# Eleven low parts of weight pieces moved from VectorE to GpSimd, with a wait of TensorE for each piece, in a two-block transformer kernel

## The chip, the cores and the metric

The kernel runs on one core of one Trainium2 chip, as one launch. The metric is the device time of the launch in microseconds. The kernel before took 1385.69 us (median of three runs, 1382.89 to 1385.78).

## What is computed

256 tokens of width 1024 go through two blocks. The first has four SwiGLU feed-forward layers (each added with factor 0.5), an mLSTM mixer after the first and an NSA attention mixer (compressed, selected and window branches over a shared K/V) after the third. The second has a forgetting-attention mixer (FOX) and a sparse attention mixer with an indexer (DSA), each followed by a layer norm. All is float32. Cut to the order of the work:

```python
x = x + 0.5 * swiglu(rmsnorm(x))              # ffn0
x = x + mlstm(rmsnorm(x) @ w_in) @ w_out      # mlstm, mlstm_out
x = x + 0.5 * swiglu(rmsnorm(x))              # ffn1
kv = rmsnorm(x) @ kv_w                        # kv, compressed during ffn2
x = x + 0.5 * swiglu(rmsnorm(x))              # ffn2
x = x + nsa(rmsnorm(x) @ w_in, kv) @ w_out    # nsa, nsa_out
x = x + 0.5 * swiglu(rmsnorm(x))              # ffn3
x = layer_norm(alpha * x + fox(x))            # fox, fox_out
x = layer_norm(alpha * x + dsa(x))            # dsa, dsa_out
```

## The kernel before

Every product with a weight is done in three products of a rounded type: a value v is split into a high part (v rounded) and a low part (v minus the high part), and x w is taken as x_lo w_hi + x_hi w_lo + x_hi w_hi (lines 658, 659, 661 in `product`, 689, 690 and 696 where the first products go ahead of the low part of x). The weights, 207 pieces of up to 128 x 2048, come through one ring of 7 slots. For each piece SyncE loads `raw` (waiting until TensorE has used the piece 7 before it), ScalarE writes the high part `whi` (`hi`, line 1472, semaphore `hi_done`), and VectorE subtracts it, `wlo = raw - whi` (`lo`, line 1987, semaphore `lo_done`). TensorE waits for `lo_done` and, after its last product with a piece, raises `used`.

The order on each engine is written out by hand. On ScalarE and on VectorE `split_to(p)` stands between the other steps and makes the high or low parts of all pieces below p that are still to be made, in order, so a low part delays what comes after it on VectorE, and a later step delays the low parts behind it. GpSimd has little to do: it issues the parameter loads at the start, masks the mLSTM decay (AFFINE_SELECT, line 623), clears pads (MEMSET, lines 627 to 640), and issues the loads of the layer-norm parameters (lines 636, 637) and of `wuk` and `wuv` (lines 641, 642).

Pieces are counted within their stage from 0. The places that the change touches:

- mlstm_out, 4 pieces. VectorE makes their low parts between the steps of the end of the mLSTM mixer: `m_weights` (lines 2291, 2293, one input in PSUM), `numerators_in` (2306 to 2309), `og_gain` (2322), `heads` (2330, eight small products per token tile), after which TensorE transposes the heads (line 705) and multiplies them with the four pieces.
- nsa_out, 4 pieces. Pieces 0 and 1 are split between the two token tiles of q: VectorE takes the root (lines 1999 to 2008) and norms q (`q_normed`, line 2505), then TensorE transposes q (line 1198). Pieces 2 and 3 are split at the end of the NSA attention.
- dsa, 12 pieces (chunks 0 to 5 of two pieces each), then dsa_out, 4 pieces (so 13 is the second piece of dsa_out). Chunks 0 to 2 are multiplied for token tile 0 while the layer norm of tile 1 (lines 2169 to 2186) still runs; in the middle of chunk 2 TensorE transposes tile 1 of h (line 678). Then come chunks 0 to 2 for tile 1, the transposes of `wuk` (1381) and of qi (1389), chunk 3, the transposes of ki and ckv (1395, 1396) and kr (1400), the index products (1411) and chunk 4. On VectorE, beside these: the rope of qi (lines 2690 to 2695), the root of ckv and the ropes of kr and ki up to the copy in line 2719, the copy of kr in line 2725, then index scores and `choose` (2750 to 2755, a top-k by repeated maxima). Chunk 5 fills TensorE while VectorE masks and scales the scores; its result goes through `silu_gate` (line 2602).

TensorE waited for a whole chunk at once (`pe.wait_ge(lo_done, end)` ahead of both its pieces) in `chunk`, `n_chunk` and the first three chunks of dsa, and for each piece by itself in the feed-forward layers and the output products.

Of the kernel before, what the change touches and what calls it, by code (L numbers as in the profile page):

```python
# [15 lines left out]
F32 = mybir.dt.float32  # L16
# [86 lines left out]
def program(nc, a, out):  # L103
# [34 lines left out]
    with ExitStack() as ctx:  # L138
# [185 lines left out]
        head_sq = sem("head_sq")  # L324
        og_ps = sem("og_ps")
        m_decay = sem("m_decay")
        og_act = sem("og_act")
# [272 lines left out]
        def _(pool):  # L600
            def load_rows(r, n, src):
                pool.dma_start(rowsb[r:r + n, :], src).then_inc(params_in, 16)

            load_rows(R_MIX, 16, a["mix_norm"].rearrange("l (k p) -> (l k) p", p=P))
            load_rows(R_KV, 8, a["kv_norm"].rearrange("(k p) -> k p", p=P))
# [13 lines left out]
            for j in range(HEADS // 2):  # L619
                pool.wait_ge(m_decay, j + 1)  # L620
                for blk in (slice(0, P), slice(256, 384)):
                    two_heads = m_E[:, 2 * j:2 * j + 2, blk]
                    pool.affine_select(out=two_heads, in_=two_heads, compare_op=ALU.is_ge, fill=0.0, base=0,
                                       pattern=[[0, 2], [1, P]], channel_multiplier=-1).then_inc(m_diag, 1)

            pool.wait_ge(h_part, h_at("mlstm_out", 1, 1))
            pool.memset(KB[:, :, :], 0.0).then_inc(pads_ready, 1)
# [4 lines left out]
            pool.memset(FL[:, :, :, :].bitcast(F32), 0.0).then_inc(pads_ready, 1)  # L632

            for i, name in enumerate(["fox_out", "dsa_out"]):
                pool.wait_ge(z_ready, 2 * (i + 2))
                pool.dma_start(LNB[:, 0, :], a["ln_g_2"][i:i + 1, :].to_broadcast([P, D])).then_inc(ln_in, 16)
                pool.dma_start(LNB[:, 1, :], a["ln_b_2"][i:i + 1, :].to_broadcast([P, D])).then_inc(ln_in, 16)
                if i == 0:
                    pool.wait_ge(h_part, h_at("ln0", 1, 1))
                    pool.memset(d_wukr[:, :, 0:32], 0.0).then_inc(pads_ready, 1)  # L640
                    pool.dma_start(d_wukr[:, :, 32:128], a["dsa_w_uk_2"].rearrange("h c n -> c h n")).then_inc(wuk_in, 16)
                    pool.dma_start(d_wuv[:, :, :], a["dsa_w_uv_2"].rearrange("h c d -> c h d")).then_inc(wuk_in, 16)


        @block.tensor
        def _(pe):
# [34 lines left out]
            def first_products(o, name, t, banks, los=(0, 0)):  # L681

                for i, (w, ks) in enumerate(banks):
                    if los[i]:
                        pe.wait_ge(lo_done, los[i])
                    pe.wait_ge(turned_hi, 4 * turns.index(name) + 2 * t + w + 1)
                    for j, (k, wh, wl) in enumerate(ks):
                        xh = XH[:, k, t * P:t * P + P]
                        mm(o, xh, wl, start=i == 0 and j == 0, stop=False, skip_group_check=True)  # L689
                        mm(o, xh, wh, start=False, stop=False, skip_group_check=True)  # L690
# [36 lines left out]
            def ffn(f, during=None):  # L727
# [25 lines left out]
                def in_products(i, t):  # L753
                    if i == 0:
                        first_half(t)
                        return
                    p = p0 + in_piece(f, i)
                    pe.wait_ge(gated, 2 * (n0 + i - 1) + t + 1)
                    for half in range(2):
                        if t == 0:  # L760
                            pe.wait_ge(lo_done, p + half + 1)
                        wh, wl = parts(p + half, 4)
                        last = product(PS[:, 4 + t, :],
                                       [(XH[:, 4 * half + k, t * P:t * P + P], XL[:, 4 * half + k, t * P:t * P + P],
                                         wh[:, k, :], wl[:, k, :]) for k in range(4)], start=half == 0, stop=half == 1)
                        if t == 1:
                            last.then_inc(used, 1)
                        elif half == 1:
                            last.then_inc(a_ready, 1)
# [8 lines left out]
                def out_step(i, between=None):  # L778
                    p = p0 + out_of(f, i)
                    pe.wait_ge(gl_done, n0 + i + 1)  # L780
                    pe.wait_ge(lo_done, p + 1)
                    last = i == NI - 1
                    out_piece(p, 0, GHz if last else GH, GLz if last else GL, i == 0, last, then_turns[name], between)
# [21 lines left out]
            def chunk(stage, c, then=None):  # L805
# [13 lines left out]
                ps = [(end - 1, 8)] if whole else [(end - 2, 4), (end - 1, 4)]  # L819
                pe.wait_ge(lo_done, end)  # L820
                if c == 0:
# [5 lines left out]
                    for t in range(NT):  # L827
                        o = PS[:, b0 + t, 0:n]
                        first_products(o, stage, t, banks)
                        if t == 0:  # L830
# [10 lines left out]
                for m in tiles:  # L841
                    for i, (p, kn) in enumerate(ps):
                        wh, wl = parts_n(p, kn, n)
                        if kind == A_CHUNK:
# [21 lines left out]
            def out_part(name, t, i):  # L866

                p = first_piece[name] + i
                if t == 0:
                    pe.wait_ge(lo_done, p + 1)  # L870
                if name == "mlstm_out":
# [177 lines left out]
            def og_products(c, t, bank):  # L1049

                n, end = stages["mlstm"][1][c][2], chunk_end("mlstm", c)
                for i, p in enumerate((end - 2, end - 1)):
                    if t == 0:
                        pe.wait_ge(lo_done, p + 1)
                    wh, wl = parts_n(p, 4, n)
# [53 lines left out]
            def blocks(kv):  # L1109
# [3 lines left out]
                for i in range(2):  # L1113
                    p = cmp_piece(kv) + i
                    pe.wait_ge(lo_done, p + 1)
                    wh, wl = parts(p, 8)
# [49 lines left out]
            def n_chunk(t, c):  # L1166

                n, end = stages["nsa"][1][c][2], chunk_end("nsa", c)
                o = PS[:, n_bank(t, c), 0:n]
                if t == 0:  # L1170
                    pe.wait_ge(lo_done, end)
                if c == 0:
                    banks = []
                    for w in range(2):
                        wh, wl = parts_n(end - 2 + w, 4, n)
                        banks.append((w, [(4 * w + k, wh[:, k, :], wl[:, k, :]) for k in range(4)]))
                    first_products(o, "nsa", t, banks)
                    for w, ks in banks:
# [3 lines left out]
                else:  # L1182
                    ps = [(end - 2, 4), (end - 1, 4)] if c == 1 else [(end - 1, 8)]
                    for i, (p, kn) in enumerate(ps):
                        wh, wl = parts_n(p, kn, n)
                        last = product(o, [(XH[:, kn * i + k, t * P:t * P + P], XL[:, kn * i + k, t * P:t * P + P],
# [170 lines left out]
            for t in range(NT):  # L1357
                for c in range(3):
                    n, end = stages["dsa"][1][c][2], chunk_end("dsa", c)
                    if t == 0:  # L1360
                        pe.wait_ge(lo_done, end)
                    for i in range(2):
                        if t == 0 and c == 2 and i == 1:
                            for w in range(2):
                                turn_h("dsa", 1, w)
                        wh, wl = parts_n(end - 2 + i, 4, n)
                        pe.wait_ge(x_ready, x_at("dsa", t, 4 * i + 3))
# [90 lines left out]
        def _(act):  # L1458
# [445 lines left out]
            x_hi("dsa", 0)  # L1904
            split_to(first + 5)
            deviation("ln0", 1)
# [66 lines left out]
        def _(dve):  # L1973
# [16 lines left out]
            def split_to(p_end):  # L1990
                for p in range(split[0], min(p_end, NP)):
                    lo(p, pieces[p][1] if pieces[p] else PIECE)
                split[0] = max(split[0], min(p_end, NP))
# [840 lines left out]
```

## Time and profile before

| | |
|---|---|
| median of three runs | 1385.69 us |
| lowest, highest | 1382.89, 1385.78 us |
| profiled execution, its own time | 1382.88 us |
| its span | 1381.2 us |
| mean granted TensorE clock | 0.979 of full speed |
| busy: TensorE, VectorE, ScalarE, GpSimd | 1302.3, 877.3, 616.9, 21.7 us |
| low parts on VectorE (line 1987) | 207, 459.4 us in all |

The profile is one execution, recorded by the hardware. Busy time is the time in which an engine works on an instruction; waiting for a semaphore is not busy. Times on the timeline count from the start of the span. In a timeline row stand the start in us, the length in us, engine, line, operation, the tile written and the tiles read, the shape, and how many equal instructions the row merges; then, in brackets, how long the engine was idle before it and who released it. The tile name `arena` covers most of the mixers' tiles.

### The profile page before, as it was taken

The numbers are of one execution on the slowest core, as the hardware profiler recorded it, in microseconds if no ns is written. First come the engines' busy times: TensorE is split into PE (matmuls) and PEld (weight loads), VectorE is DVE, ScalarE is ACT, GpSimd is POOL, SyncE is SP. The second block draws the span as 40 slices with busy tenths as digits, with TensorE's granted clock in tenths as the row PEclk, the third lists the DMA queues.
The fourth block names the chain that finished last, engine by engine and source line by source line (L and its number), as shares of the span: only waits on it lengthen the run. The fifth ranks groups of instructions, "written<-read, shape, count | busy, mean of one in ns | idle before, by whom it ended". The sixth has DMA issues, their size and how long they took to land.

```text
span 1381.2 us, 16655 instructions
## 1 busy us (share of the span) xinstructions
PE 1302.3 (94%) x6797; PEld 1099.3 (80%) x6797; DVE 877.3 (64%) x1329; ACT 616.9 (45%) x836; POOL 21.7 (2%) x36
## 2 busy tenths in 40 slices
PE   5999999879999999999999988989999999989887
PEld 4888888778788888878888865878888999868765
DVE  5555557595655557685866587665555675577664
ACT  5444446434344445534444465534443354434531
POOL 1000000100000000000000000000000000000000
PEclk9999999999999999999999999999999999999899
DMA  8665545333555555547564230355556765246001
GB/s 277 222 193 190 184 155 191 112 126 124 178 193 190 193 190 170 173 155 235 183 213 159 104 110 1 122 166 194 191 192 131 184 193 175 63 152 244 32 0 61
DMA packets 158780, 218.18 MB, mean 158 GB/s; under 512 B 8224, under 2 KB 110960, under 8 KB 158704
## 3 DMA queue, kind: packets, MB, share of 16 engines
q1 hardware_dynamic: 156848, 212.56, 47.8%
q0 software_dynamic: 1376, 3.71, 0.9%
q8 instruction: 54, 0.88, 0.3%
q10 hardware_dynamic: 480, 0.85, 0.2%
q14 instruction: 22, 0.18, 0.0%
HBM read 216.04 MB, written 1.05 MB: 157 GB/s over the span
## 4 chain that ended last, share of the span: by engine, by line
PE 82%; DVE 12%; ACT 3%; issue 2%; DMA 1%; ACTq 0%; POOL 0%; DVEq 0%
PE PS L658 23%; PE PS L659 22%; PE PS L661 22%; DVE wlo L1987 3%; PE PS L775 1%; PE PS L689 1%; PE PS L690 1%; ACT whi L1472 1%; PE PS L678 1%; PE PS L974 1%; DVE XL L2026 1%; ACT XH L1494 1%; PE PS L696 1%; PE PS L1258 1%; PE PS L1244 1%
## 5 line engine op out<-in xcount | busy, mean ns | idle before, releaser
L1987 DVE TENSOR_TENSOR wlo<-raw,whi 128x2048 fp32r<-128x2048 f32 (+3 forms) x207 | 459.4, 2230 | 125.1 <-ACT whi L1472 124.4
L1472 ACT ACTIVATE whi<-raw 128x2048 fp32r<-128x2048 f32 (+3 forms) x207 | 383.0, 1865 | 60.9 <-DMA raw<-in_fox_w_in_dram 33.5
L658 PE MATMUL PS<-whi,XL 128*128 128x512 f32 (+3 forms) x992 | 389.0, 393 | 21.6 <-DVE scr L2088 7.5
L659 PE MATMUL PS<-wlo,XH 128*128 128x512 f32 (+3 forms) x992 | 382.0, 386 | 0.0
L661 PE MATMUL PS<-whi,XH 128*128 128x512 f32 (+3 forms) x992 | 265.2, 384 | 0.0
L658 PEld LDWEIGHTS PS<-whi,XL 128*128 128x128 f32 x992 | 188.7, 190 | 58.6 <-DVE scr L2088 8.6
L659 PEld LDWEIGHTS PS<-wlo,XH 128*128 128x128 f32 x992 | 188.8, 190 | 33.2
L661 PEld LDWEIGHTS PS<-whi,XH 128*128 128x128 f32 x992 | 185.8, 190 | 35.8
L1526 ACT ACTIVATE scr<-PS,rn 128x256 f32<-128x256 f32 x88 | 41.7, 474 | 226.7 <-PE PS L661 224.0
L658 PE MATMUL PS<-whi,GL 128*128 128x512 f32 x320 | 125.4, 392 | 0.0
L659 PE MATMUL PS<-wlo,GH 128*128 128x512 f32 x320 | 124.6, 389 | 0.0
L1531 ACT ACTIVATE GH<-PS 128x512 fp32r<-128x512 f32 x40 | 23.9, 598 | 175.9 <-PE PS L775 175.9
L2085 DVE SCALAR_TENSOR_TENSOR scr<-PS,rn,scr 128x256 f32<-128x256 f32 x88 | 42.5, 482 | 91.4 <-ACT scr L1526 91.4
L661 PE MATMUL PS<-whi,GH 128*128 128x512 f32 x320 | 98.7, 390 | 0.0
L658 PE MATMUL PS<-XH,wlo 128*128 128x256 f32 x320 | 83.4, 291 | 3.3 <-DVE wlo L1987 3.3
L2094 DVE TENSOR_TENSOR GL<-PS,GH 128x512 fp32r<-128x512 f32 x40 | 27.7, 692 | 87.4 <-ACT GH L1531 87.4
L659 PE MATMUL PS<-XL,whi 128*128 128x256 f32 x320 | 82.5, 289 | 0.0
L661 PEld LDWEIGHTS PS<-whi,GH 128*128 128x128 f32 x320 | 60.1, 188 | 12.6
L659 PEld LDWEIGHTS PS<-wlo,GH 128*128 128x128 f32 x320 | 60.1, 188 | 12.1
L658 PEld LDWEIGHTS PS<-whi,GL 128*128 128x128 f32 x320 | 60.1, 188 | 12.2
L658 PEld LDWEIGHTS PS<-XH,wlo 128*128 128x128 f32 x320 | 63.5, 198 | 5.3 <-issue 5.2
L659 PEld LDWEIGHTS PS<-XL,whi 128*128 128x128 f32 x320 | 63.5, 198 | 0.0
(369 smaller groups left out, 1379.0 us busy)
## 6 DMA issues: line engine op xcount, KB each, us to landing
raw<-in_ffn_w_in_dram SPq DMA_DIRECT2D x176, 512.0 KB, 4.8
raw<-in_ffn_w_out_dram SPq DMA_DIRECT2D x88, 512.0 KB, 4.9
raw<-in_fox_w_in_dram SPq DMA_DIRECT2D x24, 512.0 KB, 7.8
raw<-in_a_w_in_dram SPq DMA_DIRECT2D x16, 512.0 KB, 4.4
raw<-in_dsa_w_in_dram SPq DMA_DIRECT2D x16, 512.0 KB, 5.6
raw<-in_kv_w_dram SPq DMA_DIRECT2D x12, 512.0 KB, 4.1
raw<-in_fox_w_in_dram SPq DMA_DIRECT2D x12, 344.0 KB, 5.2
raw<-in_a_w_out_dram SPq DMA_DIRECT2D x8, 512.0 KB, 4.8
```

The lines of the kernel that those rows point to most:

```text
L658: mm(o, xl, wh, start=start and i == 0, stop=False, skip_group_check=True)
L659: mm(o, xh, wl, start=False, stop=False, skip_group_check=True)
L661: last = mm(o, xh, wh, start=False, stop=stop and i == len(terms) - 1, skip_group_check=True)
L678: last = tr(PS[:, turn_bank(name, t, w), k * P:k * P + P], h[:, t, (4 * w + k) * P:(4 * w + k) * P + P], ident)
L689: mm(o, xh, wl, start=i == 0 and j == 0, stop=False, skip_group_check=True)
L690: mm(o, xh, wh, start=False, stop=False, skip_group_check=True)
L1472: A(whi[:, p % SLOTS, 0:n], raw[:, p % SLOTS, 0:n], ACT.Copy).then_inc(hi_done, 1)
L1526: A(ffe[:, t, :], PS[:, 4 + t, 0:FC], ACT.Sigmoid, scale=rn[:, t:t + 1]).then_inc(exp_done, 1)
L1531: A(to[:, :, :].rearrange("p k t -> p (k t)"), PS[:, 6, :], ACT.Copy).then_inc(gh_done, 1)
L1987: V.tensor_tensor(wlo[:, p % SLOTS, 0:n], raw[:, p % SLOTS, 0:n], whi[:, p % SLOTS, 0:n].bitcast(F32), ALU.subtract).then_inc(lo_done, 1)
L2085: V.scalar_tensor_tensor(out=g, in0=PS[:, 4 + t, 0:FC], scalar=rn[:, t:t + 1], in1=e, op0=ALU.mult, op1=ALU.mult).then_inc(silu_step, 1)
L2094: V.tensor_tensor(to[:, :, :], two(PS[:, 6, :]), hi_[:, :, :].bitcast(F32), ALU.subtract)\
```

## The change

GpSimd makes the low parts of eleven pieces: 1, 2 and 3 of mlstm_out, 0, 1 and 3 of nsa_out, and 5, 7, 9, 11 and 13 of dsa and dsa_out. It uses the same subtraction, from a helper `lo` of its own, and raises a semaphore of its own, `lo_pool`. VectorE's `split_to` skips these pieces. `lo_of(p)` gives, for a piece, which semaphore to wait for and its value. TensorE now waits for each piece by itself everywhere. ScalarE makes the high part of dsa piece 5 ahead of the squares of the layer norm's tile 1 instead of after them (`split_to(first + 6)`).

In GpSimd's order the mlstm_out pieces stand after the masks of the decay and ahead of the clearing of KB and VB, the nsa_out pieces ahead of the first layer-norm loads, dsa piece 5 between those loads and the wait for the first layer norm, and the last four after the loads of `wuk` and `wuv`.

```diff
+        lo_pool = sem("lo_pool")
+        pool_pieces = {"mlstm_out": (1, 2, 3), "nsa_out": (0, 1, 3), "dsa": (5, 7, 9, 11, 13)}
+        on_pool = sorted(first_piece[name] + i for name, part in pool_pieces.items() for i in part)
+
+        def lo_of(p):
+
+            if p in on_pool:
+                return lo_pool, on_pool.index(p) + 1
+            return lo_done, p + 1 - sum(1 for q in on_pool if q < p)
...
+            def lo(name, i):
+
+                p = first_piece[name] + i
+                n = pieces[p][1] if pieces[p] else PIECE
+                pool.wait_ge(hi_done, p + 1)
+                pool.tensor_tensor(wlo[:, p % SLOTS, 0:n], raw[:, p % SLOTS, 0:n], whi[:, p % SLOTS, 0:n].bitcast(F32),
+                                   ALU.subtract).then_inc(lo_pool, 1)
...
+            for i in pool_pieces["mlstm_out"]:
+                lo("mlstm_out", i)
             pool.wait_ge(h_part, h_at("mlstm_out", 1, 1))
...
+            for i in pool_pieces["nsa_out"]:
+                lo("nsa_out", i)
             for i, name in enumerate(["fox_out", "dsa_out"]):
                 pool.wait_ge(z_ready, 2 * (i + 2))
...
                 if i == 0:
+                    lo("dsa", pool_pieces["dsa"][0])
                     pool.wait_ge(h_part, h_at("ln0", 1, 1))
...
+                    for j in pool_pieces["dsa"][1:]:
+                        lo("dsa", j)
...
                 ps = [(end - 1, 8)] if whole else [(end - 2, 4), (end - 1, 4)]
-                pe.wait_ge(lo_done, end)
...
-                        first_products(o, stage, t, banks)
+                        first_products(o, stage, t, banks, (0, 0) if t else (end, 0) if whole else (end - 1, end))
...
                     for i, (p, kn) in enumerate(ps):
+                        if m == 0:
+                            pe.wait_ge(*lo_of(p))
...
             for t in range(NT):
                 for c in range(3):
                     n, end = stages["dsa"][1][c][2], chunk_end("dsa", c)
-                    if t == 0:
-                        pe.wait_ge(lo_done, end)
                     for i in range(2):
                         if t == 0 and c == 2 and i == 1:
                             for w in range(2):
                                 turn_h("dsa", 1, w)
+                        if t == 0:
+                            pe.wait_ge(*lo_of(end - 2 + i))
...
             x_hi("dsa", 0)
-            split_to(first + 5)
+            split_to(first + 6)
             deviation("ln0", 1)
...
             def split_to(p_end):
                 for p in range(split[0], min(p_end, NP)):
+                    if p in on_pool:
+                        continue
                     lo(p, pieces[p][1] if pieces[p] else PIECE)
```

`n_chunk` is changed as `chunk` is, and the other waits of TensorE for `lo_done` become waits for `lo_of` of the same piece.

## Rows read from the trace of the kernel before

**Rows 1.** The page: busy time, share of the span and instructions

```profile
PE 1302.3 (94%) x6797; PEld 1099.3 (80%) x6797; DVE 877.3 (64%) x1329; ACT 616.9 (45%) x836; POOL 21.7 (2%) x36
```

**Rows 2.** TensorE's waits: line, released by, us in total, times, longest

```profile
PE PS L658 <- DVE wlo L1987: 10.1, 3, 5.7
```

**Rows 3.** Timeline of GpSimd, mLSTM mixer, 258 to 263 us

```profile
258.32 0.76 POOL L623 TENSOR_SCALAR_AFFINE_SELECT arena<-arena 128x256 f32<-128x256 f32 x2 [221.63 <-DVE arena L2275]
...
260.38 2.01 POOL L623 TENSOR_SCALAR_AFFINE_SELECT arena<-arena 128x256 f32<-128x256 f32 x1
```

**Rows 4.** Timeline of VectorE, mLSTM mixer, 249 to 264 us

```profile
249.52 3.40 DVE L1987 TENSOR_TENSOR wlo<-raw,whi 128x1536 fp32r<-128x1536 f32 x2
...
260.37 1.76 DVE L1987 TENSOR_TENSOR wlo<-raw,whi 128x1536 fp32r<-128x1536 f32 x1 [0.42 <-ACT whi L1472]
262.05 1.96 DVE L1987 TENSOR_TENSOR wlo<-raw,whi 128x1536 fp32r<-128x1536 f32 x1
```

**Rows 5.** Timelines of ScalarE, VectorE and TensorE ahead of mlstm_out

```profile
301.15 1.90 ACT L1472 ACTIVATE whi<-raw 128x2048 fp32r<-128x2048 f32 x1
...
301.28 1.23 DVE L2322 TENSOR_TENSOR arena<-arena 128x1024 f32<-128x1024 f32 x1
...
304.77 2.18 DVE L2330 SCALAR_TENSOR_TENSOR xs<-xs,rr,arena 128x128 f32<-128x128 f32 x8
...
307.01 1.97 PE L705 MATMUL PS<-con,xs 128*128 128x128 f32 x8 [4.50 <-DVE xs L2330]
```

**Rows 6.** Timelines of ScalarE, VectorE and TensorE at the norm of q, NSA

```profile
782.62 1.90 ACT L1472 ACTIVATE whi<-raw 128x2048 fp32r<-128x2048 f32 x1
...
784.79 0.18 DVE L2008 SCALAR_TENSOR_TENSOR rr<-rt,ry 128x16 f32<-128x16 f32 x1
785.00 1.23 DVE L2505 TENSOR_TENSOR xs<-xs,rr 128x1024 f32<-128x1024 f32 x1
...
789.40 1.03 PE L1198 MATMUL PS<-con,xs 128*128 128x128 f32 x8
```

**Rows 7.** Timelines, DSA chunk 2; last a stretch's busy times, granted clock, DMA share, GB/s

```profile
1222.06 2.29 DVE L1987 TENSOR_TENSOR wlo<-raw,whi 128x2048 fp32r<-128x2048 f32 x1
...
1225.60 0.16 DVE L2174 TENSOR_TENSOR lns<-lns 128x1 f32<-128x1 f32 x1
...
1229.71 1.42 DVE L2186 SCALAR_TENSOR_TENSOR h<-xs,rr,arena 128x512 f32<-128x512 f32 x2
...
1233.50 0.80 PE L658 MATMUL PS<-whi,XL 128*128 128x512 f32 x1 [5.73 <-DVE wlo L1987]
...
1237.03 1.09 PE L661 MATMUL PS<-whi,XH 128*128 128x512 f32 x4
...
1240.68 1.08 PE L661 MATMUL PS<-whi,XH 128*128 128x512 f32 x4
...
1234.00:1238.00 4.00, 4.00 (x13) 3.09 (x13) 0.00 (x0) 0.00 (x0) 0.00 (x0) 0.63 0.70 191
```

**Rows 8.** Timelines of ScalarE, VectorE and TensorE, DSA from 1248 to 1271 us

```profile
1248.78 1.92 ACT L1472 ACTIVATE whi<-raw 128x2048 fp32r<-128x2048 f32 x1 [6.39 <-DMA raw<-in_dsa_w_in_dram]
...
1257.26 3.71 ACT L1472 ACTIVATE whi<-raw 128x2048 fp32r<-128x2048 f32 x2
...
1251.46 0.21 DVE L2690 TENSOR_TENSOR arena<-arena,con 128x64 f32<-128x64 f32 x1
...
1257.81 0.28 DVE L2708 CUSTOM_DVE_ANT_0 arena<-arena 128x128 f32<-128x128 f32 x1
...
1264.34 0.29 DVE L2719 COPY arena<-arena 128x256 f32<-128x256 f32 x1
...
1267.02 1.07 PE L661 MATMUL PS<-whi,XH 128*128 128x512 f32 x4
...
1270.17 3.80 PE L1411 MATMUL PS<-arena 64*128 64x128 f32 x24 [1.43 <-DVE arena L2725]
```

**Rows 9.** Timeline of TensorE at DSA chunk 5

```profile
1306.12 0.55 PE L658 MATMUL PS<-XH,wlo 128*128 128x256 f32 x1 [3.32 <-DVE wlo L1987]
```

More of the change, by code:

```diff
@@ L684, in first_products @@
                     if los[i]:
-                        pe.wait_ge(lo_done, los[i])
+                        pe.wait_ge(*lo_of(los[i] - 1))
                     pe.wait_ge(turned_hi, 4 * turns.index(name) + 2 * t + w + 1)
@@ L760, in in_products @@
                         if t == 0:
-                            pe.wait_ge(lo_done, p + half + 1)
+                            pe.wait_ge(*lo_of(p + half))
                         wh, wl = parts(p + half, 4)
@@ L780, in out_step @@
                     pe.wait_ge(gl_done, n0 + i + 1)
-                    pe.wait_ge(lo_done, p + 1)
+                    pe.wait_ge(*lo_of(p))
                     last = i == NI - 1
@@ L842, in chunk @@
                     for i, (p, kn) in enumerate(ps):
+                        if m == 0:
+                            pe.wait_ge(*lo_of(p))
                         wh, wl = parts_n(p, kn, n)
@@ L869, in out_part @@
                 if t == 0:
-                    pe.wait_ge(lo_done, p + 1)
+                    pe.wait_ge(*lo_of(p))
                 if name == "mlstm_out":
@@ L1053, in og_products @@
                     if t == 0:
-                        pe.wait_ge(lo_done, p + 1)
+                        pe.wait_ge(*lo_of(p))
                     wh, wl = parts_n(p, 4, n)
@@ L1114, in blocks @@
                     p = cmp_piece(kv) + i
-                    pe.wait_ge(lo_done, p + 1)
+                    pe.wait_ge(*lo_of(p))
                     wh, wl = parts(p, 8)
@@ L1176, in n_chunk @@
                         banks.append((w, [(4 * w + k, wh[:, k, :], wl[:, k, :]) for k in range(4)]))
-                    first_products(o, "nsa", t, banks)
+                    first_products(o, "nsa", t, banks, (0, 0) if t else (end - 1, end))
                     for w, ks in banks:
@@ L1184, in n_chunk @@
                     for i, (p, kn) in enumerate(ps):
+                        if t == 0:
+                            pe.wait_ge(*lo_of(p))
                         wh, wl = parts_n(p, kn, n)
@@ L1359, in _ @@
                     n, end = stages["dsa"][1][c][2], chunk_end("dsa", c)
-                    if t == 0:
-                        pe.wait_ge(lo_done, end)
                     for i in range(2):
@@ L1365, in _ @@
                                 turn_h("dsa", 1, w)
+                        if t == 0:
+                            pe.wait_ge(*lo_of(end - 2 + i))
                         wh, wl = parts_n(end - 2 + i, 4, n)
```

## The prediction

> **What bounds the kernel now.** I read the page first. TensorE is busy 94% of the span [rows 1], so only what makes TensorE wait, or lets it start earlier, can move the end. Next I read the table of waits for TensorE [rows 2]: it waits for `wlo`, the low part of a weight piece, three times in the whole kernel for 10.1 us at that line. Two of the three lie in the DSA stage, 5.73 us before the products at 1233.50 [rows 7] and 3.32 us before those at 1306.12 [rows 9]; the third is in ffn0, which the change leaves alone. VectorE makes the low part of every piece; the change takes eleven from it, and nine of these have no TensorE wait behind them. Then I read the timelines around each of the eleven, for what VectorE and TensorE do while GpSimd would be at work.
>
> **What GpSimd and VectorE do to each other.** The trace shows it once, clearly. Two AFFINE_SELECTs of 128x256 took 0.76 us together at 258.32, 0.40 each with a start every 0.36, but the one at 260.38 took 2.01 us [rows 3]. VectorE's subtraction of two SBUF tensors ran from 260.37 to 262.13. GpSimd ended at 262.39, 0.26 us later, and the next VectorE subtraction, recorded from 262.05, took 1.96 us where two of the same shape took 3.40 us together, 1.70 each [rows 4]. So the two engines excluded each other for whole instructions, and took turns: GpSimd got in between two VectorE instructions that stood back to back. Of the 0.40 us some 0.13 comes before the exclusion (0.40 less 0.26). The Trainium skill (SBUF — State Buffer, "Who interferes with whom") says the same: a VectorE instruction with two SBUF inputs and a GpSimd instruction that reads SBUF lock each other out, the later one for all of the earlier. By that rule, the trace agrees, a GpSimd subtraction stops every two-input VectorE instruction that comes up while it runs, and the change would lose time; without it, it would gain, as in rival (a).
>
> **Price of one GpSimd subtraction.** No row shows one. From below: VectorE's own, 2.29 us [rows 7]. From above: by the 0.36 us from start to start of the pair [rows 3], eight times (2048/256) and doubled for the second input, 5.8 us. I take 4.5: the 0.27 us of the 0.40 that follow the dispatch make 1.05 ns an element for one input, twice that for two, times 2048, is 4.3, plus 0.13. It is nearest to the rows of GpSimd itself. The Trainium skill (GPSIMD Engine Reference, "Elementwise — side-by-side cycle accounting") gives 4497 ns for a two-input add of this size; the sum would be the same.
>
> **Part 1, mlstm_out (pieces 1, 2, 3).** Removed: three subtractions of VectorE. The first brings the chain to the heads forward by about 1 us, after which it waits for TensorE; piece 2 runs beside `og_gain` of tile 0 (line 2322, two SBUF inputs) and takes most of that back. I set the two at nothing. Piece 3 becomes ready on ScalarE at 303.05; ScalarE waits there for TensorE, which is the microsecond ahead, so about 302.1; `og_gain` of tile 1 is then just running [rows 5], GpSimd follows it at about 303.1 and holds to 307.6. The eight head products of tile 1 (line 2330, two SBUF inputs, start 304.77) wait for that: they start 2.9 us late, and TensorE's transposes at 307.01, which already wait 4.50 us for them, come 2.9 us late. TensorE has nothing else queued there. Sum **+2.9**; between -1.0 (no exclusion) and +4.3 (GpSimd in ahead of `og_gain`).
>
> **Part 2, nsa_out (pieces 0, 1, 3).** ScalarE has piece 0 ready at 784.52 [rows 6]. GpSimd would be in at about 784.7, VectorE's last small step of the root (line 2008, two SBUF inputs) is due at 784.79 and the norm of q (line 2505) at 785.00. GpSimd holds to 789.2, VectorE does its 0.18 us step, GpSimd takes its turn with piece 1 to 793.9, and the norm ends at 795.1 instead of 786.2. TensorE asks for it at 789.40: **+5.7**. All hangs on 0.3 us: if GpSimd comes later than 785.00, the norm is ahead of it and the cost is nothing. Piece 3 hides behind TensorE's products of pieces 0 to 2. The two subtractions that VectorE loses here stood before a wait of it, so nothing is gained.
>
> **Part 3, dsa piece 5, with its own wait and the earlier high part.** Before, TensorE stood from 1227.77 to 1233.50, for both halves of chunk 2. Now it does the half that is ready (piece 4, from 1222.06 [rows 7], done at 1224.35) in 2.7 us of the gap, and then waits for the layer norm of tile 1 (line 2186, first half written at 1230.4). GpSimd starts piece 5 at 1224.35 and holds to 1228.85; the layer norm's line 2174 (two SBUF inputs, 1225.60) starts 3.25 us late and all behind it. TensorE resumes at 1233.7, turns h, and does the second half in 4.6 us at the lower clock, which is what the first half took after the old wait (1233.50 to 1238.12; the granted clock is 0.63 from 1234 to 1238, part at 1.2 and part at 2.4 GHz). Chunk 2 ends about 1239.6 (1233.7, a transpose of 0.9 and 4.6, with part of it overlapped) where it ended at 1241.76: **-2.2**. Without exclusion: -6.
>
> **Part 4, dsa pieces 7, 9, 11.** Piece 7 is ready on ScalarE at 1250.7 [rows 8], now 2.2 earlier, so GpSimd holds the port from 1248.7 to 1253.2, and the rope of qi (line 2690, now 1251.46, with part 3 at 1249.3) waits: 1.5 of the 2.2 us are lost, **+1.5**. Pieces 9 and 11: ScalarE makes high parts 9 to 11 back to back from 1257.26 [rows 8] (the row has the first two; 9 is the first, 11 the third), so GpSimd has two subtractions nearly end to end, 1258.6 to 1263.1 and, after one VectorE step, to 1267.8. From 1257.8 to 1264.3 [rows 8] VectorE runs the chain of small two-input instructions (root and ropes) that ends in line 2719 at 1264.34. 5.2 us of it are left at 1258.6, so it ends at 1273. TensorE finishes chunk 3 at 1267.4 and needs it: with the one subtraction left to VectorE there (2.3 us) and the copies up to line 2725 (1.1 us) its index products start at 1276.4, not 1270.17. This step alone costs **+6.9** (6.2 over the old time plus the 0.7 that parts 3 and 4 still had).
>
> **Part 5, the wait at chunk 5.** VectorE subtracted piece 11 just before, and TensorE waited 3.32 us [rows 9]. GpSimd has it ready long before. Piece 13 then holds the port during `choose(1)` and costs 0.5 at the gate that follows. **-2.8.**
>
> **Sum.** +2.9 +5.7 -2.2 +1.5 +6.9 -2.8 = +12.0 us. The profiled execution took 1382.9 us (span 1381.2 and 1.7 around it), so 1394.9; it is 2.8 below the median of the runs shown, 1385.69. As I don't know which of the two the next runs will be like, I forecast in the middle, 1384.3 + 12.0, rounded to **1396**. Its bounds: at 5.8 us a piece each of the seven blocks counted above is 1.3 us longer, +9; a lower clock of TensorE after the two new waits of over 5 us would add 1.8 each, the difference of the two halves in part 3 (4.6 and 2.8). At 2.3 us a piece the blocks nearly close: +0.6 +1.2 -4.4 +2 -2.8 = -3.4, which is inside the range below. With 4 to 5 us a piece the case has 1390 to 1405.
>
> **Rivals.** (a) *No exclusion for long GpSimd instructions*: the port is shared in small portions, so the blocks vanish. Then -1.0, 0, -6, -1.0 (VectorE has one subtraction fewer before line 2725, where TensorE waited 1.43 us [rows 8]) and -3.3, sum -11.3: **1373**. For it: the exclusion of VectorE by GpSimd is only shown for 0.26 us. Against it: GpSimd was shut out for all 1.76 us of a VectorE instruction. It is the case on the faster side. (b) *The double blocks miss*: GpSimd enters 0.3 us later at 785 and the pair 9 and 11 does not get a second turn. Then +2.9, 0, -0.7, +2.3, -2.8: **1386**, no change. It decides at line 2505. (c) *One of the two double blocks happens*: +6 to +7, **1391**. (d) *GpSimd takes well over 5.8 us*: pieces come late for TensorE itself and it ends above 1405.
>
> **How the numbers follow.** The forecast's case 0.42, (c) 0.18, (d) 0.04, (b) 0.11, (a) 0.25. A measurement of this kernel tells some 0.2%, 2.8 us, from no change, so (b) is half "same", and of (c) nearly all is slower: slower 0.65, same 0.09, faster 0.26. The range has to leave out no more than 0.2; the upper cases from 1384 hold 0.72, so it reaches into (a) to its slower half: 1375 to 1405. The forecast's case alone has 1390 to 1405.
>
> **What would show it.** In the profile after: eleven GpSimd TENSOR_TENSOR of 4.3 to 4.7 us; records of lines 2505 (or 2008), 2174, 2330 and the small steps before 2719 that last 3 us and more where they took 0.2 to 1.2; TensorE waiting for line 2505 near 789, and for line 2719 near 1268; the waits for `wlo` gone from the DSA stage. If two-input VectorE instructions keep their times beside a running GpSimd subtraction, the forecast is wrong and (a) holds.

## Result, and the profile after

The changed kernel takes 1398.07 us (median of ten runs, 1391.16 to 1403.32) against 1388.28 (ten runs, 1382.89 to 1392.70): ratio **1.0075, interval 1.0049 to 1.0102**. It is slower, by 10 us. The profiled execution took 1394.36 us, its span is 1392.6, its mean granted clock 0.972. The prediction had 1396 (1375 to 1405).

The first row of the page of the kernel after answers to [rows 1], and the row of costs beside it is GpSimd's:

```profile
PE 1305.6 (94%) x6797; PEld 1102.0 (79%) x6797; DVE 884.0 (63%) x1318; ACT 617.4 (44%) x836; POOL 73.7 (5%) x47
...
L619 POOL TENSOR_TENSOR wlo<-raw,whi 128x2048 fp32r<-128x2048 f32 x11 | 51.8, 4721 | 334.8 <-ACT whi L1498 334.8
```

VectorE lost eleven subtractions (207 at 459.4 us before, 196 at 436.6 now, so 22.8 us of work) and is busy for 6.7 us *more*. So its other instructions take 29.5 us longer (6.7 + 22.8). The timelines show which. First GpSimd's eleven subtractions (seven rows; two of them hold a pair):

```profile
278.28 4.90 POOL L619 TENSOR_TENSOR wlo<-raw,whi 128x2048 fp32r<-128x2048 f32 x1 [1.65 <-ACT whi L1498]
287.32 4.55 POOL L619 TENSOR_TENSOR wlo<-raw,whi 128x2048 fp32r<-128x2048 f32 x1 [4.14 <-ACT whi L1498]
302.36 5.04 POOL L619 TENSOR_TENSOR wlo<-raw,whi 128x2048 fp32r<-128x2048 f32 x1 [10.48 <-ACT whi L1498]
...
786.14 9.06 POOL L619 TENSOR_TENSOR wlo<-raw,whi 128x2048 fp32r<-128x2048 f32 x2 [160.45 <-ACT whi L1498]
...
1232.85 4.90 POOL L619 TENSOR_TENSOR wlo<-raw,whi 128x2048 fp32r<-128x2048 f32 x1 [17.89 <-ACT whi L1498]
...
1265.47 9.18 POOL L619 TENSOR_TENSOR wlo<-raw,whi 128x2048 fp32r<-128x2048 f32 x2 [5.18 <-ACT whi L1498]
...
1322.59 4.65 POOL L619 TENSOR_TENSOR wlo<-raw,whi 128x2048 fp32r<-128x2048 f32 x1 [47.93 <-ACT whi L1498]
```

(Two more, of pieces nsa_out 3 and dsa 7, start at 871.84 and 1255.69.) Then VectorE's timeline in the same stretches. Each row answers to one of [rows 5 to 8], where the same instruction took 2.18, 0.18, 1.23, 0.16 and 0.21 us:

```profile
305.05 4.33 DVE L2358 SCALAR_TENSOR_TENSOR xs<-xs,rr,arena 128x128 f32<-128x128 f32 x8
...
786.15 4.63 DVE L2036 SCALAR_TENSOR_TENSOR rr<-rt,ry 128x16 f32<-128x16 f32 x1
790.81 5.47 DVE L2533 TENSOR_TENSOR xs<-xs,rr 128x1024 f32<-128x1024 f32 x1
...
1234.54 3.24 DVE L2202 TENSOR_TENSOR lns<-lns 128x1 f32<-128x1 f32 x1
...
1256.31 4.07 DVE L2718 TENSOR_TENSOR arena<-arena,con 128x64 f32<-128x64 f32 x1
...
1265.45 0.16 DVE L2033 TENSOR_TENSOR rt<-rt,rv 128x2 f32<-128x2 f32 x1
1265.64 4.48 DVE L2035 SCALAR_TENSOR_TENSOR ry<-rt,ry 128x2 f32<-128x2 f32 x1
1270.16 4.51 DVE L2032 TENSOR_TENSOR rt<-ry 128x2 f32<-128x2 f32 x1
1274.70 0.16 DVE L2033 TENSOR_TENSOR rt<-rt,rv 128x2 f32<-128x2 f32 x1
```

An instruction on one element a partition lasts 3.24 us, and it ends at 1237.78 when GpSimd's subtraction ends at 1237.75. Two steps on two elements last 4.5 us each (their neighbours 0.16), one per subtraction of GpSimd's pair: the engines took turns. Steps with one input in PSUM are not held: beside the subtraction at 278.28 VectorE's records of line 2319 last 0.47 us and those of line 2321 0.34, as in the kernel before. Beside the subtraction at 1322.59 VectorE runs the repeated maxima of `choose(1)`, and none of its records there is longer than before.

Last, TensorE's timeline, to be read against [rows 5, 6, 7, 8, 9]:

```profile
309.43 1.97 PE L730 MATMUL PS<-con,xs 128*128 128x128 f32 x8 [5.66 <-DVE xs L2358]
...
796.33 1.97 PE L1224 MATMUL PS<-con,xs 128*128 128x128 f32 x8 [5.44 <-DVE xs L2533]
...
1242.53 1.32 PE L703 MATMUL PS<-con,h 128*128 128x128 f32 x8 [3.07 <-DVE h L2214]
...
1279.56 0.48 PE L1421 MATMUL PS<-con,arena 128*128 128x128 f32 x1 [5.27 <-DVE arena L2747]
...
1282.85 6.51 PE L1437 MATMUL PS<-arena 64*128 64x128 f32 x24 [1.75 <-DVE arena L2753]
...
1318.62 0.58 PE L683 MATMUL PS<-XH,wlo 128*128 128x256 f32 x1
```

The waits for `wlo` in the DSA stage are gone (that of 5.73 and that of 3.32 us), and waits of 5.44, 3.07 and 5.27 us for VectorE's own chains stand in their place. TensorE's waits add up to 77.0 us, 69.1 before.

The next table takes an instruction that both profiles have and gives how much later it starts after the change; the last column is what was added since the row above:

| landmark | before | after | shift | of this step |
|---|---|---|---|---|
| transposes of the heads, tile 1 | 307.01 | 309.43 | +2.4 | +2.4 |
| sum of squares of q, tile 0 | 781.15 | 782.51 | +1.4 | -1.0 |
| transposes of q | 789.40 | 796.33 | +6.9 | +5.6 |
| transposes of h, tile 0, DSA | 1217.17 | 1226.11 | +8.9 | +2.0 |
| end of chunk 2, tile 0 | 1241.76 | 1246.61 | +4.9 | -4.1 |
| last group of chunk 3 | 1267.02 | 1273.22 | +6.2 | +1.4 |
| index products | 1270.17 | 1282.85 | +12.7 | +6.5 |
| scores of DSA | 1294.26 | 1310.84 | +16.6 | +3.9 |
| chunk 5 | 1306.12 | 1318.62 | +12.5 | -4.1 |
| end of the span | 1381.2 | 1392.6 | +11.4 | -1.1 |

### The profile page after: what moved, and what is told of

Read it like the earlier page. It is cut to its first block, busy times and chain, and to the rows that moved or that the text cites. A ratio compares the mean times of both kernels' runs of the same rounds, so it can differ in the third digit from the quotient of the medians.

```text
span 1392.6 us, 16661 instructions
## 1 busy us (share of the span) xinstructions
PE 1305.6 (94%) x6797; PEld 1102.0 (79%) x6797; DVE 884.0 (63%) x1318; ACT 617.4 (44%) x836; POOL 73.7 (5%) x47
## 3 DMA queue, kind: packets, MB, share of 16 engines
q0 software_dynamic: 1376, 3.71, 0.9%
## 4 chain that ended last, share of the span: by engine, by line
PE 79%; DVE 14%; ACT 3%; issue 2%; DMA 1%; ACTq 0%; POOL 0%; DVEq 0%
PE PS L683 22%; PE PS L684 22%; PE PS L686 21%; DVE wlo L2013 3%; PE PS L800 1%; ACT whi L1498 1%; PE PS L714 1%; PE PS L715 1%; PE PS L703 1%; PE PS L1000 1%; DVE XL L2054 1%; DVE rt L2032 1%; ACT XH L1520 1%; PE PS L1284 1%; PE PS L1469 1%
## 5 line engine op out<-in xcount | busy, mean ns | idle before, releaser
L2013 DVE TENSOR_TENSOR wlo<-raw,whi 128x2048 fp32r<-128x2048 f32 (+4 forms) x196 | 436.6, 2238 | 125.9 <-ACT whi L1498 125.3
L683 PE MATMUL PS<-whi,XL 128*128 128x512 f32 (+3 forms) x992 | 388.6, 392 | 14.8 <-DVE scr L2116 7.4
L686 PEld LDWEIGHTS PS<-whi,GH 128*128 128x128 f32 x320 | 60.1, 188 | 12.7
L619 POOL TENSOR_TENSOR wlo<-raw,whi 128x2048 fp32r<-128x2048 f32 x11 | 51.8, 4721 | 334.8 <-ACT whi L1498 334.8
```

The lines of the kernel that those rows point to most:

```text
L619: pool.tensor_tensor(wlo[:, p % SLOTS, 0:n], raw[:, p % SLOTS, 0:n], whi[:, p % SLOTS, 0:n].bitcast(F32), ALU.subtract).then_inc(lo_pool, 1)
L683: mm(o, xl, wh, start=start and i == 0, stop=False, skip_group_check=True)
L686: last = mm(o, xh, wh, start=False, stop=stop and i == len(terms) - 1, skip_group_check=True)
L2013: V.tensor_tensor(wlo[:, p % SLOTS, 0:n], raw[:, p % SLOTS, 0:n], whi[:, p % SLOTS, 0:n].bitcast(F32), ALU.subtract).then_inc(lo_done, 1)
```

## Experiments

The theory is that of the prediction: a GpSimd instruction that reads SBUF and a VectorE instruction with two SBUF inputs exclude each other for whole instructions and take turns. The rivals are that the waits per piece or ScalarE's new order cost the time, that any work of GpSimd does, and that the pieces come late. "The change" is the changed kernel of each diff.

**Taking all pieces from GpSimd, or all but one stage's.**

```diff
-        pool_pieces = {"mlstm_out": (1, 2, 3), "nsa_out": (0, 1, 3), "dsa": (5, 7, 9, 11, 13)}
+        pool_pieces = {"mlstm_out": (), "nsa_out": (), "dsa": ()}
```

The three others each keep one stage's tuple of the first line.

> The changed kernel with no piece on GpSimd: VectorE makes all 207 low parts again, TensorE waits for each piece on its own and ScalarE makes dsa piece 5 ahead of the squares. Theory (whole instructions of the two engines exclude each other): nothing holds VectorE here, lines 2358, 2533 and 2747 go at their old length, and TensorE does the first half of chunk 2 in the old gap of 5.73 us and part of chunk 5 in the old gap of 3.32 us: 3 to 5 us faster than before, about 1381. Rival (the many waits or the new order on ScalarE cost the time): as slow as the changed kernel, about 1398.

> As the run with no piece on GpSimd, but with pieces 1, 2, 3 of mlstm_out on it. Theory: the last eight head products (line 2358) start about 2 us late and TensorE's transposes with them; 2.4 us more than the run without any, less than 3. Rival (GpSimd's blocks on VectorE are hidden and the clock or the waits make the loss): no difference to it.

> As the run with no piece on GpSimd, but with pieces 0, 1, 3 of nsa_out on it. Theory: the last step of the root (line 2036) and the norm of q (line 2533) are blocked one after the other; TensorE waits over 5 us where it waited for nothing and then runs at a lower clock for a while: 5.7 to 7 us more than the run without any. If GpSimd comes in 0.3 us later the block of the root goes and the norm is ahead of it: 0 more.

> As the run with no piece on GpSimd, but with pieces 5, 7, 9, 11, 13 of dsa on it. Theory: pieces 9 and 11 hold up the small instructions ahead of line 2747, TensorE waits 5 us for it; against the run with no piece on GpSimd, which has the gain of the waits already, 7 to 10 us more. Rival (the loss is made in the earlier stages and only carried here): 2 more at most. The three parts together should give what the whole change gives.

Measured against 28 runs of before (median 1388.04):

| kernel | median us | ratio | interval |
|---|---|---|---|
| no piece on GpSimd | 1377.54 | 0.9921 | 0.9902 to 0.9940 |
| mlstm_out only | 1386.99 | 0.9997 | 0.9981 to 1.0013 |
| nsa_out only | 1392.35 | 1.0027 | 1.0010 to 1.0044 |
| dsa only | 1393.06 | 1.0027 | 1.0007 to 1.0048 |

Against the kernel with no piece on GpSimd each stage's pieces cost time, and the waits alone gain it: 10.5 us, where I expected 3 to 5. The timelines say how the waits gain: TensorE does the first half of chunk 2 and the transposes of h inside the old gap, and of chunk 5 the products of the piece that is ready (piece 10). TensorE's timeline of the kernel with no piece on GpSimd, against the 5.73 and 3.32 us of [rows 7, 9]:

```profile
1235.62 0.50 PE L686 MATMUL PS<-whi,XL 128*128 128x512 f32 x1 [1.67 <-DVE wlo L2016]
...
1309.20 0.58 PE L686 MATMUL PS<-XH,wlo 128*128 128x256 f32 x1 [0.37 <-DVE wlo L2016]
```

All of TensorE's waits fall from 69.1 to 61.8 us, by 7.3. The waits of the three others are those of the change, stage by stage: 7.6 us at the heads (mlstm_out only; 5.3 without), 5.2 at the norm of q (nsa_out only), 5.3 at line 2750 (dsa only; that is line 2747 of the change, three lines down in this file). So the causes are where the table of shifts has them. The *sizes* are not: I expected under 3, 5.7 to 7 and 7 to 10 us more than the run without any, and got 9.5, 14.8 and 15.5. I had also expected the three to add up to what the whole change costs over that run (1398.07 less 1377.54, 20.5 us); they make 39.8.

**The change again, GpSimd writing zeros, GpSimd in quiet places, ScalarE's old order.**

The zeros:

```diff
-                pool.tensor_tensor(wlo[:, p % SLOTS, 0:n], raw[:, p % SLOTS, 0:n], whi[:, p % SLOTS, 0:n].bitcast(F32),
-                                   ALU.subtract).then_inc(lo_pool, 1)
+                k = 2 * on_pool.index(p)
+                pool.memset(wlo[:, p % SLOTS, 0:n].bitcast(F32), 0.0).then_inc(pool_step, 1)
+                pool.wait_ge(pool_step, k + 1)
+                pool.memset(wlo[:, p % SLOTS, 0:n].bitcast(F32), 0.0).then_inc(pool_step, 1)
+                pool.wait_ge(pool_step, k + 2)
+                pool.memset(wlo[:, p % SLOTS, 0:n // 2].bitcast(F32), 0.0).then_inc(lo_pool, 1)
```

The quiet places:

```diff
-        pool_pieces = {"mlstm_out": (1, 2, 3), "nsa_out": (0, 1, 3), "dsa": (5, 7, 9, 11, 13)}
+        pool_pieces = {"mlstm_out": (1,), "nsa_out": (0, 1), "dsa": (11, 13)}
...
+            pool.wait_ge(q_norm, 1)
             for i in pool_pieces["nsa_out"]:
                 lo("nsa_out", i)
...
+                        pool.wait_ge(chosen, 1 if j == 11 else 2)
                         lo("dsa", j)
...
+                        V.max(d_m8[:, :], work).then_inc(chosen, 1)
+                        dve.wait_ge(chosen, t + 1)
```

The old order, on top of no piece on GpSimd:

```diff
-            split_to(first + 6)
+            split_to(first + 5)
             deviation("ln0", 1)
```

> The changed kernel itself, to have it against the same runs as the others. If the three parts run alone (9, 15 and 15 us over the run with no piece on GpSimd) added up, it would take 1.02 times the time before, 1417. If they don't (each part run alone held something that they have in common, like the clock at the start of the kernel), it takes what it took, 1.0075 times, about 1398.

> The changed kernel, but GpSimd fills the low part of its eleven pieces with zeros in three writes (2048, 2048 and 1024 elements a partition; 1.82, 1.82 and 0.96 us by the clears of FH and VB) instead of the subtraction: as long, 4.6 us, but it reads no SBUF. The low parts of these eleven weight pieces are left out of the result. Theory (the exclusion is by reading SBUF in GpSimd): lines 2036, 2202, 2358, 2533 and the small steps ahead of 2747 keep their old times of 0.2 to 2.2 us, TensorE's waits for them go, and the time is 1371 to 1376, the sum of rival (a). Rival (any work of GpSimd holds VectorE, or a write does): the records stay at 3 to 5 us and the time at about 1398.

> Each subtraction of GpSimd is put where VectorE has no instruction with two SBUF inputs for as long as it runs: piece 1 of mlstm_out as it was, pieces 0 and 1 of nsa_out after the norm of q (a wait for q_norm), pieces 11 and 13 of dsa beside the repeated maxima of choose(0) and choose(1) (a wait for its first maximum); the other six are VectorE's again. Theory: nothing is blocked though GpSimd works as long per piece; as the run with no piece on GpSimd to 2 us, 1375 to 1380, and all subtractions of 4.5 us. Rival (GpSimd's work costs something wherever it stands, by the waits or the clock): 1385 or more.

> No piece on GpSimd, TensorE waits per piece, and ScalarE makes dsa piece 5 after the squares again, as before. Theory: the gain of the first run is the half chunks that TensorE does inside the two old gaps, and VectorE subtracts piece 5 after the layer norm in any case: the same as the first run, 0.992 of before, 1377 to 1380. Rival (the new order on ScalarE makes the gain): half of it goes, 1383.

Measured against 25 runs of before (median 1387.97):

| kernel | median us | ratio | interval |
|---|---|---|---|
| the change again | 1399.30 | 1.0091 | 1.0069 to 1.0112 |
| zeros in place of the subtraction | 1378.59 | 0.9948 | 0.9922 to 0.9973 |
| quiet places | 1381.08 | 0.9956 | 0.9941 to 0.9972 |
| no piece on GpSimd, old order | 1383.50 | 0.9970 | 0.9957 to 0.9983 |

*The zeros decide it.* (This kernel leaves the low parts of eleven pieces out of its result, so it is a probe and no alternative.) GpSimd is at work for as long (4.6 us a piece) at the same places, and 20.7 us are gone (1399.30 less 1378.59); 1378.59 is 2.6 above the top of what I had expected (1371 to 1376). The timelines of this kernel, VectorE's rows and GpSimd's beside them: the head products keep their 2.18 us, the norm of q its 1.23 and a step of the layer norm its 1.29 (1.28 before), each with a write running beside it:

```profile
304.74 2.18 DVE L2366 SCALAR_TENSOR_TENSOR xs<-xs,rr,arena 128x128 f32<-128x128 f32 x8
...
304.93 1.80 POOL L623 MEMSET wlo<- 128x2048 f32 x1
...
783.79 1.23 DVE L2541 TENSOR_TENSOR xs<-xs,rr 128x1024 f32<-128x1024 f32 x1
...
783.96 1.80 POOL L621 MEMSET wlo<- 128x2048 f32 x1 [160.94 <-ACT whi L1506]
...
1229.03 1.81 POOL L623 MEMSET wlo<- 128x2048 f32 x1
...
1229.26 1.29 DVE L2215 SCALAR_TENSOR_TENSOR xs<-h,lns,arena 128x1024 f32<-128x1024 f32 x1
...
1261.86 1.81 POOL L623 MEMSET wlo<- 128x2048 f32 x1
...
1262.09 1.60 DVE L2754 TENSOR_SCALAR arena<-arena 128x16 f32<-128x16 f32 x1
1262.18 1.65 DVE L2755 COPY arena<-arena 128x256 f32<-128x256 f32 x1
```

So it is the reading: two-input instructions of VectorE keep their times beside a GpSimd that only writes. VectorE's busy time says the same for the whole kernel: its instructions other than low parts take 29.5 us longer than before in the profile of the change and 4.3 us longer with the zeros. The last two rows are the exception, of another kind: they have *one* input, they took 0.17 and 0.29 us in the kernel before, and both end just after the write does (1263.67). A pair of such instructions at 1256.92 (line 2750, 128x128) is held in the same way, 2.19 us where it took 0.48. TensorE waits 2.3 us for the copy at line 2761 that follows, 1.4 before [rows 8].

*The quiet places bear it out from the other side.* GpSimd's five subtractions take 4.57 to 4.90 us as in the change, and VectorE's instructions other than low parts take 0.7 us longer than before, in all. The norm of q is at 784.68 with its 1.23 us and GpSimd's pair right behind it, and at `choose(0)`, `choose(1)` the maxima run beside the subtraction at the lengths they had (GpSimd's timeline, then two steps of VectorE in the middle of the first of the two):

```profile
785.99 9.14 POOL L620 TENSOR_TENSOR wlo<-raw,whi 128x2048 fp32r<-128x2048 f32 x2 [161.94 <-DVE xs L2538]
...
1278.00 4.60 POOL L620 TENSOR_TENSOR wlo<-raw,whi 128x2048 fp32r<-128x2048 f32 x1 [39.64 <-DVE d_m L2786]
...
1279.77 0.29 DVE L2789 MAX8 d_m<-d_work 128x8 f32<-128x128 f32 x1
...
1280.18 0.28 DVE L2790 MATCH_REPLACE8 d_work<-d_m,d_work 128x128 f32<-128x128 f32 x1
```

The time, 1381.08, is 1.1 above what I had expected (1375 to 1380) and lies among the kernels without GpSimd (1377.54 to 1384.64), not below them: TensorE had nothing left to gain from these five pieces (waits 60.2 us against 61.8).

*The change again* repeats 1.0075 with 1.0091; the stages' costs do not add up to 1.02. Its profile shows how close the race was on which part 2 of the prediction's sum stood. In the profile of the change GpSimd began piece 0 at 786.14 and the root's last step came at 786.15, hence two blocks. Here, by VectorE's timeline, the step was through in time and the norm came up at the moment GpSimd started (786.09), so only one subtraction went ahead of it:

```profile
785.89 0.17 DVE L2036 SCALAR_TENSOR_TENSOR rr<-rt,ry 128x16 f32<-128x16 f32 x1
786.10 5.70 DVE L2533 TENSOR_TENSOR xs<-xs,rr 128x1024 f32<-128x1024 f32 x1
```

TensorE waits 1.2 us instead of 5.4. Both ways occur, and 0.26 us in VectorE's chain decides. This execution was nevertheless longer (span 1398.8), at a lower mean clock (0.967, 0.972 in the other).

*The old order* came out at 0.9970, as the rival had it (half of the gain of the waits given back) and not as I expected (0.992), though TensorE's waits in both kernels are the same (61.3 and 61.8 us). So both were run again.

**One piece fewer beside the chain, and the two orders again.** The first leaves 9 out of the tuple for dsa: `"dsa": (5, 7, 11, 13)`. The others are the two kernels without GpSimd, unchanged.

> The changed kernel with dsa piece 9 given back to VectorE. GpSimd still has piece 11 beside the small steps ahead of line 2747 (from about 3.7 us later, when ScalarE has its high part), so one block of 4.3 us is left of two. Theory: the steps end 4.3 us earlier and TensorE's wait at line 1421 falls from 5.3 to 1 us, but VectorE now has two subtractions of 2.3 us ahead of line 2753, so TensorE waits there instead and 2 us are gained, 1.000 to 1.007 of before. Rival (the two blocks are not in turn, the loss there is that of the first): nothing is gained or 4.5 us are, with no new wait at line 1437.

> The kernel with no piece on GpSimd once more, beside the one with ScalarE's old order. The two had the same waits of TensorE, line by line. Theory: they are the same, both 0.992 to 0.997 of before, and what they differed in (0.992 and 0.997) was how often TensorE's clock was at its lower level. Rival (ScalarE's order gives half of the gain): this one again at 0.992, the other at 0.997.

> The kernel with no piece on GpSimd and ScalarE's old order once more. Theory: the same as its partner of this call. Rival: 5 us slower than it.

Measured against 24 runs of before (median 1387.96):

| kernel | median us | ratio | interval |
|---|---|---|---|
| the change without piece 9 | 1396.01 | 1.0067 | 1.0040 to 1.0094 |
| no piece on GpSimd | 1382.90 | 0.9943 | 0.9918 to 0.9969 |
| no piece on GpSimd, old order | 1384.64 | 0.9958 | 0.9929 to 0.9987 |

The two orders are the same within their intervals; the first run of the one (0.9921, six runs) was low. The mean ratio of the four measurements of the two orders is 0.9948: **the waits per piece alone gain some 7 us**, and no effect of ScalarE's order can be told. TensorE's timeline without piece 9:

```profile
1279.42 0.33 PE L1424 MATMUL PS<-con,arena 128*128 128x128 f32 x1 [1.00 <-DVE arena L2750]
1284.91 6.51 PE L1440 MATMUL PS<-arena 64*128 64x128 f32 x24 [4.62 <-DVE arena L2756]
```

The wait of 5.27 us falls to 1.00 and that behind it rises from 1.75 to 4.62, as expected: one block less, one subtraction of VectorE more ahead of the copy of kr. VectorE's small step caught there lasted 4.58 us. The 2 us of gain fit (1396.01, the change 1398.07 and 1399.30), but the interval also holds no gain, and this profile had one block at the norm of q, not two. The waits show the mechanism, the time alone would not.

## Why the prediction was right, and where it was not

**The exclusion** held in every case that I had counted but one (the maxima of `choose(1)`, part 5), and so rivals (a) and (b) fell: (a) because a 128x1 step lasted 3.24 us, (b) because the pair 9 and 11 did get its second turn. Rival (c), one double block only, is what the repeated run shows at the norm of q, at 1.0091 all the same. Rival (d) fell with the **price**, 4.5 us forecast and 4.55 to 5.04 measured (those of over 4.8 us start while VectorE is in a two-input instruction, as at 302.36 and 1232.85, so their records seem to hold part of that wait). The Trainium skill (SBUF — State Buffer, "Who interferes with whom") has all three cases seen here: two inputs against a GpSimd that reads, two inputs free against one that only writes, and a one-input copy or `tensor_scalar` in a two-port mode held by it all the same. The traces agree with the first two; in the third the copy and the `tensor_scalar` were held (1.65 and 1.60 us for 0.29 and 0.17), but that they ran in such a mode no run shows.

The parts are those of the prediction's sum, forecast in brackets and then measured. **Part 1** (+2.9): +2.4. **Part 2** (+5.7): +5.6 in this profile, and a further 2.0 up to the DSA stage. The 2.0 are there 9 us after the new wait, where the granted clock was 0.55 (796 to 801 us); I had named this and left it out of the sum. That they are still there at the DSA stage looks like chance: 1.5 of them come back at once, where the kernel before ran at 0.75 from 801 to 806 and the changed one at 1.00, and 1.4 are lost again from 1120 to 1130, at 0.83 against 1.00, far from any piece on GpSimd. **Part 4** (+1.5 and +6.9): +1.4 and +6.5, and again a low clock behind the wait, +3.9: 0.50 from 1280 to 1290, so the index products that took 3.80 us [rows 8] took 6.51.

**Part 3** (-2.2): -4.1. TensorE resumed when I had said (1242.53 less the 8.9 us of shift is 1233.6; forecast 1233.7). The term that failed is "the second half in 4.6 us at the lower clock". It took 2.8, at the full clock. The shorter gap (3.07 us, not 5.73) does not account for it: in the second profile of the change the gap is 3.08 us, the clock is 0.67 from 1242 to 1247, and the same products take 4.4 us (1243.59 to 1248.01), near what I had put in. With no piece on GpSimd they take 4.4 us too, after 1.67 us of gap. So the extra gain of this part is luck. TensorE's timeline in the second profile of the change:

```profile
1242.52 1.32 PE L703 MATMUL PS<-con,h 128*128 128x128 f32 x8 [3.08 <-DVE h L2214]
1243.59 0.66 PE L683 MATMUL PS<-whi,XL 128*128 128x512 f32 x1
...
1248.01 0.33 PE L683 MATMUL PS<-whi,XL 128*128 128x372 f32 x1
```

**Part 5** (-2.8): -4.1. Of these 3.3 are the wait; the other 0.8 are the score products ahead of it, of which more ran at the full clock (7.8 us, 8.5 before). The 0.5 us at the gate for piece 13 were wrong, as the maxima are not held. More than the size, the **reason** was wrong. I had written that GpSimd has piece 11 ready long before, and so the wait goes. The kernel without GpSimd has 0.37 us of that wait left, as TensorE does the products of piece 10 meanwhile. The gain of parts 3 and 5 is that of the waits per piece; GpSimd adds the last 0.4 us to the gain of part 5 and takes 1.4 from that of part 3 (TensorE waits 3.07 us for the layer norm, which piece 5 holds up, where it waits 1.67 for `wlo` without).

So the sum of +12.0 came out as +11.4 on the profiled executions with errors against each other: 2.0 + 3.9 us of low clock not counted, 1.9 and 1.3 us of gain missed in parts 3 and 5, about 1 us too much in the other parts, and -1.0 and -1.1 at two places that no part claims. That they cancel is luck, and so is the closeness of the time: the 1384.3 us that I started from were 4.0 below the median of the ten runs of before (1388.28), and the 12.0 were 2.2 above the 9.8 by which the medians differ. What was right for its reason is the sign, the exclusion, its price and its places. Put as the experiments have it: waits per piece -7 us, GpSimd +18 to +20 us (1.0075 and 1.0091 less 0.9948, of 1388). The change joined a gain to a larger loss, and no kernel with a piece on GpSimd came out faster than the waits alone (0.9948), which beat both the kernel before and the changed one.

**What stays open** is the size of one stage's pieces alone. The three came out at +7, +11 and +11 us over the mean of the kernels without GpSimd (0.9997, 1.0027, 1.0027 against 0.9948), 29 together, where the three at once cost 18 to 20. The waits that they add to the profiles are 1.4, 5.0 and 7.6 us. The granted clocks of all runs say where most of the excess lies. As an estimate, a low clock costs a run its span times one less its granted clock (too much where TensorE waits anyway); the means over all runs of the experiments, and for the change the ten of the result too:

| kernel | runs | span, us | by low clock | rest |
|---|---|---|---|---|
| before | 77 | 1386.3 | 37.4 | 1348.9 |
| no piece on GpSimd, both orders | 43 | 1379.6 | 34.6 | 1345.0 |
| mlstm_out only | 12 | 1386.2 | 42.6 | 1343.6 |
| nsa_out only | 12 | 1389.8 | 42.2 | 1347.7 |
| dsa only | 11 | 1391.0 | 40.1 | 1350.9 |
| the change | 16 | 1396.7 | 44.7 | 1352.0 |

Against the kernels with no piece on GpSimd the rests of the three stages (-1.4, +2.7, +5.9) add up to what the change has (+7.2 and +7.0). The low clock does not add up: +8.0, +7.6 and +5.5 are 21, and the change has +10.1. So by this estimate more than half of what GpSimd costs in the change, and 7 of the 10 us by which it is slower than before, are time at a low clock, which the prediction's sum put at nothing. The split is rough (the change without piece 9 has 39.7 and 1355.4 in seven runs, a larger rest than the change itself), and why each stage alone meets nearly as much low clock as all three was not found.

## What to carry over

Before giving GpSimd elementwise work, list VectorE's instructions with two SBUF inputs in the stretch where it would run, however small: each can cost the whole GpSimd instruction (4.5 us for a 0.16 us step), and two GpSimd instructions end to end cost a chain of small steps twice. Put such work by a semaphore behind VectorE's last two-input step and beside products out of PSUM, maxima or idle time. And try the finer waits by themselves first: here they were worth 7 us, and the work moved for their sake cost more than twice that.

## What was not expected of the hardware

- A one-input copy (128x256) and a `tensor_scalar` (128x16), both from SBUF to SBUF, lasted 1.65 and 1.60 us beside a GpSimd instruction that only writes, while two-input instructions beside such writes kept their times (2.18, 1.23 and 1.29 us).
- MAX8 and MATCH_REPLACE8 are not held by a GpSimd subtraction (0.29 and 0.28 us beside it).
- Two executions of one program can differ by which engine comes first by 0.01 us (786.14 and 786.15), and so by 4 us of TensorE's wait.
- Executions with equal waits can differ by where the clock is low. The kernels with no piece on GpSimd, with TensorE's waits between 61.0 and 61.8 us in four profiles, had spans from 1374.9 to 1383.8 us. Those two ends are one kernel (old order): the longer one is 1.1 us early at the norm of q, 4.0 late at the index products (granted clock 0.67 from 800 to 825 us, 0.93 in the other) and 8.8 late at chunk 5 (0.91 and 1.00 from 1250 to 1290, 0.80 and 0.90 from 1290 to 1325). The mean clock of a span alone does not tell it: two of the four have 0.976, and spans of 1374.9 and 1380.8 us.
- The length of the gap before it does not settle whether a stretch runs at the low clock: behind the same gap of 3.1 us the second half of chunk 2 took 2.8 us in one profile of the change (granted clock 1.00) and 4.4 in the other (0.67).
